# A two-block sequence model: the mixer's GELU and gate tiles earlier in the attention rounds

## The reference

```python
z = rmsnorm(h, norm_mix[i]) @ w_in[i]
q, kc, vc, ksl, vsl, kw, vw, g, u = jnp.split(z, split_at, axis=-1)
...
o_nsa = nsa_attention(q, kc, ..., gates, ...)       # 8 heads; compressed, selected, window
o_s5 = s5_mixer(u, ...)
h = h + jnp.concatenate([o_nsa, o_s5], axis=-1) @ w_out[i]

def s5_mixer(u, ..., w_glu, b_glu):
    ...                                             # a linear recurrence gives y
    y = jax.nn.gelu(y.reshape(B, L, S5_WIDTH))
    out = y * jax.nn.sigmoid(y @ w_glu + b_glu)
```

## Time and profile before

| | |
|---|---|
| median of 3 runs | 1968.04 us (1967.81 to 1971.5) |
| profiled execution | 1969.36 us, its span 1967.6 us |
| PE busy | 1920.7 us, 98% |
| DVE busy | 1185.2 us, 60% |
| ACT busy | 816.6 us, 42% |
| POOL busy | 339.5 us, 17% |
| mean granted clock of PE | 0.987 |

### The profile page before, as it was taken

How to read it: one execution, slowest core, us unless ns; L and a number is a source line. 1 busy time by engine, 2 the same in 40 slices (tenths; PEclk the granted TensorE clock), 3 DMA queues, 4 the chain that set the end, 5 groups by cost and what they waited for, 6 DMA issues and landing times.

```text
span 1967.6 us, 22513 instructions
## 1 busy us (share of the span) xinstructions
PE 1920.7 (98%) x9002; PEld 1496.8 (76%) x9002; DVE 1185.2 (60%) x1521; ACT 816.6 (42%) x1210; POOL 339.5 (17%) x329
## 2 busy tenths in 40 slices
PE   8999999999998999999999999999999999999997
PEld 6787888777544778888888877876788878776786
DVE  5748344577964456656656787836753659457732
ACT  5322333311565342222333448555642466455621
POOL 2000000136320101001011211504201014114001
PEclk9999999999998999999999899999999899999998
DMA  6322323222101245545532322220222322221321
GB/s 221 108 82 87 118 90 104 92 70 102 44 1 64 75 169 183 202 161 195 183 114 92 112 96 76 86 94 33 84 88 97 107 75 86 65 86 33 100 93 43
DMA packets 53464, 197.27 MB, mean 100 GB/s; under 512 B 6000, under 2 KB 6512, under 8 KB 52848
## 3 DMA queue, kind: packets, MB, share of 16 engines
q1 hardware_dynamic: 43200, 160.55, 24.3%
q0 software_dynamic: 7648, 29.10, 4.5%
q10 hardware_dynamic: 2512, 6.18, 1.0%
HBM read 192.67 MB, written 2.10 MB: 99 GB/s over the span
## 4 chain that ended last, share of the span: by engine, by line
PE 81%; DVE 10%; ACT 3%; POOL 3%; issue 2%; DMA 0%; ACTq 0%; POOLq 0%; DVEq 0%
PE PS L624 80%; DVE WLO L1720 2%; DVE AR L1752 1%; ACT WHI L1241 1%; DVE TMP L2327 1%; DVE AR L2075 1%; PE PS L883 1%; POOL ACC L2385 1%; POOL AR L2422 1%; DVE AR L1723 0%; DVE AR L1981 0%; DVE H L2153 0%; ACT HX L1420 0%; DMA H<-in_xT 0%; DVE RS L1738 0%
## 5 line engine op out<-in xcount | busy, mean ns | idle before, releaser
L624 PE MATMUL PS<-HNH,WHI 128*128 128x512 f32 x1632 | 657.0, 403 | 8.9 <-ACT HNH L1272 8.8
L1720 DVE TENSOR_TENSOR WLO<-RAW,WHI 128x1024 fp32r<-128x1024 f32 (+1 forms) x272 | 365.2, 1348 | 469.2 <-ACT WHI L1241 469.1
L624 PE MATMUL PS<-HNH,WLO 128*128 128x512 f32 x1632 | 639.9, 392 | 4.7 <-DVE WLO L1720 4.6
L1241 ACT ACTIVATE WHI<-RAW 128x1024 fp32r<-128x1024 f32 (+1 forms) x272 | 296.1, 1094 | 589.8 <-PE PS L624 539.8
L624 PE MATMUL PS<-HNL,WHI 128*128 128x512 f32 x1632 | 434.8, 389 | 0.1
L624 PEld LDWEIGHTS PS<-HNH,WHI 128*128 128x128 f32 x1632 | 308.7, 189 | 85.7 <-issue 19.7
L624 PEld LDWEIGHTS PS<-HNH,WLO 128*128 128x128 f32 x1632 | 308.6, 189 | 79.5 <-issue 9.3
L624 PEld LDWEIGHTS PS<-HNL,WHI 128*128 128x128 f32 x1632 | 306.4, 188 | 64.6 <-DVE HNL L1723 1.0
L2385 POOL TENSOR_TENSOR ACC<-ACC,SQ 128x512 f32<-128x512 f32 x46 | 61.6, 1339 | 796.1 <-ACT SQ L1256 795.2
L624 PE MATMUL PS<-AR 32*128 32x256 f32 (+14 forms) x852 | 160.7, 408 | 4.3 <-POOL AR L2422 2.0
L624 PE MATMUL PS<-HIDH,WLO 128*128 128x512 f32 x352 | 137.1, 389 | 1.3 <-DVE WLO L1720 1.3
(11 more groups left out here) (320 smaller groups left out, 2275.7 us busy)
## 6 DMA issues: line engine op xcount, KB each, us to landing
RAW<-in_w_in SPq DMA_DIRECT2D x80, 512.0 KB, 3.5
AR<-in_w_ada POOLq DMA_DIRECT2D x48, 512.0 KB, 3.8
RAW<-in_w13a SPq DMA_DIRECT2D x44, 512.0 KB, 3.4
RAW<-in_w13b SPq DMA_DIRECT2D x44, 512.0 KB, 3.5
RAW<-in_w_out SPq DMA_DIRECT2D x40, 512.0 KB, 3.5
RAW<-in_w2a SPq DMA_DIRECT2D x16, 704.0 KB, 4.1
RAW<-in_w2b SPq DMA_DIRECT2D x16, 704.0 KB, 4.4
RAW<-in_w_inA SPq DMA_DIRECT2D x12, 512.0 KB, 3.5
```

The costliest lines, as they stand in the source:

```text
L624: return pe.matmul(o, l, r, start=start, stop=stop, skip_group_check=True)
L1241: act.activation(hi_of(name, i), raw_of(name, i), ACT.Copy).then_inc(*HI.up(name, i))
L1720: dve.tensor_tensor(lo_of(name, i), raw_of(name, i), f32(hi_of(name, i)), S_).then_inc(*LO.up(name, i))
```

## The change

Only numbers in `mix_order` change. The GELU goes from round 23 to round 16. The gate's tiles 0 to 3 go from rounds 25, 26, 27, 28 to rounds 18, 20, 22, 24, with their tanh. The products `s5_out` go from rounds 29 and 30 to 25 and 26, the low parts 4 to 7 from rounds 30 and 31 to 26 and 27. `o_part` and the low parts 0 to 2 stay in rounds 28 and 29. The calls of `convert` move too: tiles 0 to 3 of the output matrix were split in rounds 21, 24, 27 and 30 and are now split in rounds 17, 19, 23 and 27. The instructions themselves are the same; POOL's and SP's rows are the same in both kernels, though the moments at which SP's loads may start follow PE's reads and the splits.

```diff
@@ -287,12 +287,12 @@
-        if n == 23:
+        if n == 16:
             assert next(s5, None) is None
             yield ("gelu",)
-        if 24 < n < 29:
-            yield "glu", n - 25
-        if n in (2, 3, 21, 24, 25, 27, 28, 30):
+        if n in (18, 20, 22, 24):
+            yield "glu", n // 2 - 9
+        if n in (2, 3, 17, 19, 21, 23, 25, 27):
             yield ("convert",)
@@ -300,12 +300,12 @@
-        if n in (29, 30):
-            yield "s5_out", 2 * n - 58
-            yield "s5_out", 2 * n - 57
-        if n in (30, 31):
-            yield "low", 2 * n - 56
-            yield "low", 2 * n - 55
+        if n in (25, 26):
+            yield "s5_out", 2 * n - 50
+            yield "s5_out", 2 * n - 49
+        if n in (26, 27):
+            yield "low", 2 * n - 48
+            yield "low", 2 * n - 47
```

## The result

The changed kernel took 1973.18 us in the median of 20 runs (1969.03 to 1975.2), the kernel before, beside it on the same chip, 1968.21 us (1965.9 to 1972.2, 20 runs). The ratio is 1.0019 with a 95% interval from 1.0013 to 1.0025, so 3.7 us slower (2.6 to 4.9); the two medians themselves are 5.0 us apart. The profiled execution of the changed kernel took 1972.21 us, its span 1970.5 us, at a mean granted clock of 0.987; 16 of the 20 runs had 0.984 to 0.986.

What follows compares the result with a forecast made beforehand. PE was taken as busy nearly all the time, with a few waits and low clock behind them. +3.47 +1.75 -4.12 -1.3 -7.2 +9.4 +2.0 = +4.0 us on the median 1968.04 gave 1972.0 us, range 1964 to 1976.5.

Steps and rivals of the forecast that it cites:

- The GELU: Round 18: `values` waits for copies behind the GELU's table load and four activations on ACT, +3.47 us.
- The clock behind the wait: After the new GELU wait PE runs at 1.2 GHz for some microseconds, +1.75 us; bounds nothing and twice that.
- The two short waits: Between rounds 18 and 24 two PE waits of 0.33 us vanish, with the slower flips -1.3 us.
- The drain: A skill page's 1.38 us per table load, not seen before the GELU; would lengthen old and new wait alike, difference unchanged.
- The old wait: PE's 2.37 us wait at the first gate tile after the GELU goes, with 1.75 of clock: -4.12 us.
- `out_s5`: First output matrix products with the mixer's half: waits and clock go, 15.57 becomes 8.34 us, -7.2.
- The end: Rounds 25 to 31 lose gate-tile cover, gain mixer work; `values` starts at 23.5 instead of 14.1, +9.4 us (bounds 6, 11).
- The clock behind the last hole: PE at half speed after the last new wait, before `values` in the end, +2.0 us; bounds 0 and 4.
- the three named waits: PE waits before the flips of (3,1,3), the shares of (3,1) and behind `o_part`, 7 to 9.5 us in all.
- Rival 1: DVE gets through rounds 26 to 28 beside PE, both end terms fall away: -7.4, 1960.6 us; chance 0.15.
- rival 3: Clock stays low longer, another 1.75 us behind the GELU and 3 in rounds 30 and 31: 1976.8 us; chance 0.14.
- Rival 2: Waits as summed, but PE stays at 2.4 GHz in both new places: +0.25, 1968.3 us; chance 0.23.

Runs made afterwards that it cites:

- experiment in round 17: Changed kernel with the GELU in round 17 instead of 16 and the first gate tile in 19 instead of 18; ratio to the kernel before 0.9993.
- the two cures: Changed kernel with GELU in round 17, first gate tile in 19, `o_part`, low parts 0-2, last split in 32, low parts 4-7 in 30, 31; 1959.7 us.
- late tail: Changed kernel with `o_part`, low parts 0 to 2 and the split of output matrix tile 3 in round 32; ratio to the kernel before 0.9991.
- outputs back: Changed kernel with `s5_out` back in rounds 29 and 30 and low parts 4 to 7 in 30 and 31; ratio to the kernel before 1.0012.
- late tail and late low parts: Changed kernel with `o_part`, low parts 0-2 and last split in round 32, low parts 4-7 in rounds 30 and 31; ratio to before 0.9985.

## Why the prediction was right

The forecast was 1972.0 for the median, which came to 1973.18, and 1973.4 for a profiled execution, which came to 1972.21. The sum was +4.0; in the profile it is +3.25 over the stretch, by the ratio +3.7. The forecast lay on the bound that it gave for what can be told from no change, 3.9 us; the measured 3.7 lies there too, and with 20 runs of each its interval, 2.6 to 4.9, does not reach zero.

**The GELU.** The wait is 3.75 us, 3.50 more than the 0.25 that stood there; the forecast was 3.47, the table load and the four activations. The reading that decided it was that `values` had already been waiting for these very copies, so that no cover was left. The second table load, at 572.55, costs PE nothing, as said. The clock behind the wait cost 1.03 us in `values` (2.76 for 1.73), 0.25 in two transposes, 0.30 in the scores, 1.6 in all against 1.75. The two short waits gave back 0.48 us each, not 0.33 (from the product before the flips to the next instruction, 0.61 and 0.62 before, 0.13 after). With them the piece is +3.59 for +4.24. The experiment in round 17 shows the mechanism: the same instructions behind the copies cost 1.0 us.

**The drain.** The Trainium skill (ScalarE: Activation LUTs, What ACT_TABLE_LOAD costs) adds about 1.38 us to each load. The load starts at 568.08 and takes 1.28, the first GELU starts at 569.38, 0.02 us later: no such drain shows in either trace, before or after, where the function behind a load waits for no other engine, and the wait of 3.75 leaves no room for one. The measurement decides.

**The old wait.** Its piece shrank by 4.50 us: 2.37 of waiting, 1.75 of clock and the 0.32 of slow flips that the forecast has among its short waits.

**`out_s5`.** 8.45 for 8.34; both waits and their clock went, as the three equal tiles promised.

**The end.** With 0 at 606.29, the moments can be laid beside each other: maxima of (3,1,3) at 13.2 (forecast 13.4), flips at 14.8 (15.0), shares at 20.0 (20.2), `values` at 23.2 (23.5), end of `out_s5` at 40.35 (23.5 + 6.3 + 2.0 + 8.34 = 40.1). The replay of two queues with the durations of the old profile was good to 0.3 us over 23. Its undisturbed 14.1 should be 14.2, since two of the three gate tiles that it takes off are 3.49 us long, not 3.58. Against the row before, which has a wait of 0.17 there, `values` is 8.9 us later. The clock behind the last hole cost 2.4 us (8.66 from `values` to `out_s5`, 6.24 before) for 2.0, so 9.4 + 2.0 came out as 8.9 + 2.4.

**What the prediction got only half.** Three points behind the right number:

- It named three waits in the end; there are four. The bank wait of 1.25 us before the scores at 618.46 was not foreseen. It cost nothing more, since the flips behind it were waiting for a later event anyway: lateness against the undisturbed order counts once. The waits sum to 7.09, while `values` is some 9 us late; 1.5 of the rest is PE at 1.2 GHz between the holes (flips 1.94 us for 1.04, scores 1.22 for 0.70). That is no cost of its own: in the round 17 experiment the shares took 0.89 us longer and the hole behind them was 0.88 shorter, as the prediction had it. The forecast's number of 9.4 was for the lateness and was right. Its sentence that the three named waits would be 7 to 9.5 us was not: they sum to 5.84 and reach 7 only with the fourth. The hole before the shares was 1.75 us where it had said 3.
- Rival 1 was decided by a threshold, about 9 us of DVE's work between two marks, and 12.4 was called such work. It is time that passes: 1.8 of it, from 14.9 to 16.7, is DVE standing before the split in the prediction's own replay, and in the trace 9.6 of 12.1 us are busy. With the mixer's 4.3 us (1.28 + 1.51 + 1.51) taken out again, 12.4 become 8.1 (7.9 in the trace, 5.7 busy), and the threshold would have had these waits gone. They are not: 1.51 before the shares, 2.14 before `values`. DVE's own wait of 1.79 us for ACT's half of the split, and ACT's 1.66 us of `o_part` ahead of a copy, hold PE just as well. What counts is the chain from exponential to split on ACT, to split on DVE, to shares, and not the sum of one engine's work. So the loss of the gate tiles' cover weighs more, and the arrival of the mixer's work less, than the prediction's words had it: 4.3 of the waits are there without that work, 2.8 came with it.
- The clock terms came out as 1.6 and 2.4 for 1.75 and 2.0. That is partly luck: the second execution of the same kernel had 6.8 us of low clock around the GELU's hole, as long as in the old `out_s5`, which is rival 3 in length though not in price (0.8 us more, not 1.75, since a part lay in the hole). Rival 2, that the clock would hold, did not come in any run with the wait of 3.75 us.

Rival 1 as a time, 1960.6, is near what the two cures reached, 1959.7, by coincidence: its sum has the GELU's 5.2 us still in it and no wait in the end, while the cures left 1.0 and 1.8 us of the two.

## To carry to other kernels

A block of work that is moved on an in-order engine should stand behind the results that the next engine asks for first, not ahead of them: the same 3.47 us of GELU cost 5.1 us, waits and clock, ahead of two copies and 1.0 us behind them. That is no promise for every such place: behind the copies of round 21 it still cost 2.6 us of waits. When long PE work is moved away, look at what it covered, moved or not; here 4.3 of the 7.1 us of new waits remained when the steps that the change had brought in were taken out again. Queues of two engines can be replayed from the old profile to a few tenths of a microsecond, if each wait of one for the other is put in as well as the durations.

## What the runs showed of the hardware

**The low clock is not set by the wait alone.** The same wait of 3.75 us came with 3.4 us at 0.50 in the changed kernel, in the two kernels with a late tail and with the outputs back, and with 6.8 in the second profile of the changed kernel and with the GELU alone in round 16, where the clock fell some 1.8 us before the hole ended. A wait of 1.66 us before the flips of (3,1,3) had 0.50 behind it with the late tail, and 1.00 with both cures. A window of each, from 1.6 and 1.3 us behind the start of the flips:

```profile
620.00:623.00 3.00, 3.00 (x24) 2.16 (x24) 1.71 (x4) 2.34 (x9) 0.00 (x0) 0.50 0.02 5
```

```profile
617.00:620.00 3.00, 3.00 (x31) 1.77 (x30) 1.88 (x5) 2.64 (x10) 0.00 (x0) 1.00 0.02 5
```

The second of these kernels had no other wait over 1 us from 560 us on, the first had the one of 3.74 us, 47 us before. Whether that or chance decides, the runs do not tell. The Trainium skill (TensorE: Matmul & The Clock Gate, What's actually happening) says of the start of a kernel that the point at which the clock changes varies because the monitor runs freely. These runs show such a variation in the middle of a kernel, not its cause; it moved the clock term of the GELU from 1.6 to about 2.4 us.

**The mean clock goes with much of the spread between runs.** Of the kernel with the late tail and late low parts the three runs nearest the median, 1966.6 us, had a mean clock of 0.987, the fastest, 1958.87, had 0.992. At half speed a microsecond costs half a microsecond, so 0.005 of 1967 us stands for about 10 us by my estimate; the two are 7.7 apart, twice the effect under study. The order is not strict: the changed kernel took 1969.03 us at 0.986 and 1970.59 us at 0.987. One profiled execution therefore tells where the waits are, and only several timed runs what a kernel takes.
